# The last expert's down product in output halves, with its scatter and the last norm's first statistics between them

## What is computed

```python
def clamped_swiglu(a, u):
    a = jnp.minimum(a, SWIGLU_LIMIT)
    u = jnp.clip(u, -SWIGLU_LIMIT, SWIGLU_LIMIT)
    return a * jax.nn.sigmoid(SWIGLU_ALPHA * a) * (u + 1.0)
...
        hid = clamped_swiglu(xb @ w_gate[e] + b_gate[e], xb @ w_up[e] + b_up[e])
        yb = hid @ w_down[e] + b_down[e]
        return (yb * gt[:, None].astype(yb.dtype)).astype(t.dtype)
...
    # then, on alpha * h + moe(h), over the last axis of 1024:
    return ((tf - mu) * lax.rsqrt(var + LN_EPS) * g + b).astype(t.dtype)
```

## Time and profile before

| | us |
|---|---|
| median of 3 runs | 1060.38 (1060.24 to 1061.34) |
| span of the profiled execution | 1058.6 |
| TensorE busy | 1023.2 (97%) |
| VectorE, ScalarE, GpSimd busy | 229.8, 146.2, 28.0 |
| mean rate of all transfers | 403 GB/s |

### The profile page before, as it was taken

One profiled execution on the slowest core, in us unless ns is written; L12 is line 12 of the kernel. 1 busy time (PEld: TensorE's weight loads), 2 busy tenths in 40 slices (PEclk: granted clock), 3 DMA queues, 4 the chain that ended last, 5 costly groups with the idle time before them and its releaser, 6 DMA issues.

```text
span 1058.6 us, 12174 instructions
## 1 busy us (share of the span) xinstructions
PE 1023.2 (97%) x5124; PEld 450.5 (43%) x5124; DVE 229.8 (22%) x502; ACT 146.2 (14%) x358; POOL 28.0 (3%) x52
## 2 busy tenths in 40 slices
PE   9999999999999999999999999999999999999997
PEld 8888764333333333333333333333333333233332
DVE  5453572111111111111111112211111111111113
ACT  4311331111111111001110111111111111011102
POOL 1230100000000000000000000000000000000000
PEclk9999999999999999999999999999999999999999
DMA  9894689999999999999999999999999999999995
GB/s 315 272 414 178 210 320 407 429 427 433 431 433 430 430 428 435 433 431 432 428 435 433 428 428 432 434 430 427 431 434 431 430 431 431 436 426 425 427 418 219
DMA packets 40011, 426.21 MB, mean 403 GB/s; under 512 B 6922, under 2 KB 19347, under 8 KB 23204
## 3 DMA queue, kind: packets, MB, share of 16 engines
q1 hardware_dynamic: 37796, 423.85, 95.3%
q10 hardware_dynamic: 2176, 1.80, 0.7%
HBM read 424.59 MB, written 1.05 MB: 402 GB/s over the span
## 4 chain that ended last, share of the span: by engine, by line
PE 68%; DMA 29%; ACT 1%; DVE 1%; issue 0%; SPq 0%; POOL 0%; DVEq 0%; ACTq 0%
PE bank L1209 29%; DMA ring<-in_moe_w_up 18%; PE bank L1260 15%; DMA ring<-in_moe_w_gate 11%; PE bank L1181 4%; PE bank L1189 4%; PE bank L865 3%; PE bank L880 2%; PE bank L1055 2%; PE bank L1043 1%; PE bank L997 1%; PE bank L1251 1%; PE bank L1129 1%; PE bank L958 1%; PE bank L1063 1%; PE bank L1229 1%
## 5 line engine op out<-in xcount | busy, mean ns | idle before, releaser
L1209 PE MATMUL bank<-ring,arena 128*64 128x512 f32 x1988 | 447.9, 603 | 23.5 <-DMA ring<-in_moe_w_up 20.0
L1209 PEld LDWEIGHTS bank<-ring,arena 128*64 128x64 f32 x1988 | 142.4, 139 | 298.6 <-issue 256.8
L1260 PE MATMUL bank<-ring,arena 128*64 128x512 f32 x1024 | 226.8, 595 | 1.5 <-issue 1.5
L1260 PEld LDWEIGHTS bank<-ring,arena 128*64 128x64 f32 x1024 | 71.5, 137 | 151.7 <-issue 150.2
L1654 DVE COPY arena<-bank 128x512 f32<-128x512 f32 x32 | 22.1, 692 | 326.1 <-PE bank L1260 326.1
L746 ACT ACTIVATE arena<-arena 128x512 f32<-128x512 f32 x32 | 20.1, 629 | 450.9 <-DVE arena L1641 450.9
L1189 PE MATMUL bank<-arena 64*128 64x512 f32 x256 | 72.0, 640 | 0.9 <-DVE arena L1654 0.9
L1181 PEld LDWEIGHTS bank<-arena 128*128 128x128 f32 x480 | 58.8, 196 | 22.8 <-issue 22.8
L1648 DVE TENSOR_SCALAR arena<-bank 128x512 f32<-128x512 f32 x32 | 22.1, 691 | 210.2 <-PE bank L1209 210.2
L757 ACT ACTIVATE arena<-bank 128x512 f32<-128x512 f32 x32 | 19.1, 598 | 337.3 <-PE bank L1251 337.3
L1181 PE MATMUL bank<-arena 128*128 128x128 f32 x480 | 64.5, 288 | 0.0
(11 more groups left out here) (293 smaller groups left out, 518.5 us busy)
## 6 DMA issues: line engine op xcount, KB each, us to landing
ring<-in_moe_w_down SPq DMA_DIRECT2D x25, 4096.0 KB, 28.8
ring<-in_moe_w_gate SPq DMA_DIRECT2D x24, 4096.0 KB, 25.0
ring<-in_moe_w_up SPq DMA_DIRECT2D x24, 4096.0 KB, 27.8
ring<-in_moe_w_gate SPq DMA_DIRECT2D x10, 2048.0 KB, 22.8
ring<-in_moe_w_up SPq DMA_DIRECT2D x10, 2048.0 KB, 15.1
ring<-in_moe_w_down SPq DMA_DIRECT2D x10, 2048.0 KB, 17.3
ring<-in_w_in SPq DMA_DIRECT2D x12, 1024.0 KB, 11.8
ring<-in_moe_w_gate SPq DMA_DIRECT2D x8, 1024.0 KB, 18.2
```

The source lines that it names most:

```text
L1209: ins = mm(b[h * SL:(h + 1) * SL, :], (xA[pp], xB)[q][:, k, par * SL:(par + 1) * SL], columns(unit_at(m, kt), h), start=False, stop=kt == ...
L1260: ins = mm(bank[6][h * SL:(h + 1) * SL, :], hidT[:, kt % 4, (kt // 4) * SL:(kt // 4 + 1) * SL], unit_at(2, kt)[:, h * 512:(h + 1) * 512], ...
```

## The change

The diff, cut to what acts:

```diff
-LAST_PIECES = ((0, 2, 4, 6, 8), (0, 2, 4, 6, 7, 8), (0, 2, 4, 6, 7, 8))
+LAST_PIECES = ((0, 2, 4, 6, 8), (0, 2, 4, 6, 7, 8))
+LAST_DOWN = ((0, 3, 0, D), (3, 6, 0, 512), (6, 8, 0, 512), (3, 5, 512, D), (5, 7, 512, D), (7, 8, 512, D))
...
+                        for c, (k0, k1, c0, c1) in enumerate(LAST_DOWN):
+                            sp.dma_start(slot(s)[:, k0:k1, c0:c1], piece_src(e, m, slice(k0, k1), slice(c0, c1))).then_inc(
+                                w_landed[LAST_DOWN_AT + c] if c else landed[s], 16)
...
-            pool.wait_ge(rstd2, 1)
-            y, v, w = rstd[:, 0:1], vtmp[:, 0:1], vnew[:, 0:1]
-            link(nc.gpsimd.tensor_tensor(w, y, y, ALU.mult))
-            link(nc.gpsimd.tensor_tensor(w, w, v, ALU.mult))
-            link(nc.gpsimd.tensor_scalar(w, w, -0.5, 1.5, ALU.mult, ALU.add))
-            link(nc.gpsimd.tensor_tensor(y, y, w, ALU.mult))
-            nc.gpsimd.tensor_scalar(diag[:, :], ident[:, :], y, None, ALU.mult).then_inc(diag_ok, 1)
+            def root(y, v, n):
+                return nc.gpsimd.tensor_tensor(y, v, mhalf[0:n, :], ALU.pow)
+
+            pool.wait_ge(var2, 1)
+            link(root(rstd[:, 0:1], vtmp[:, 0:1], P))
+            nc.gpsimd.tensor_scalar(diag[:, :], ident[:, :], rstd[:, 0:1], None, ALU.mult).then_inc(diag_ok, 1)
+            pool.wait_ge(var2, 2)
+            root(rstd[:, 1:2], vtmp[:, 1:2], P).then_inc(rstd2, 1)
...
+                if last:
+                    act.wait_ge(d_ps, n)
+                    for q in range(2):
+                        act.wait_ge(hidT_ps, n + q + 1)
+                        nc.scalar.activation(hidT[:, 2 * q:2 * q + 2, :].rearrange("p c n -> p (c n)"), bank[4 + q][:, 0:2 * P],
+                                             ACT.Copy).then_inc(hidT_ok, 1)
+                    act.wait_ge(d_ps, n + 2)
+                    nc.scalar.activation(y_s[:, 256:512], bank[7][:, 0:256], ACT.Copy).then_inc(yd_ok, 1)
+                    return
...
-            nc.scalar.preload_act_table_set("natural_log_exp_and_others")
-            act.wait_ge(scat[1], nx + NE)
-            def mean_part(h):
...
+            def last_scatter(n, hh, par):
+                pe.wait_ge(yd_ok, n + 1 + hh)
+                for turn in range(2):
+                    for t in range(NT):
+                        p = t ^ turn
+                        ins = mm(bank[2 * t + hh][:, p * 256:(p + 1) * 256], selGT[par][p * SL:(p + 1) * SL, t * P:(t + 1) * P],
+                                 y_s[p * SL:(p + 1) * SL, hh * 256:(hh + 1) * 256], start=False, stop=False, skip_group_check=True)
+                        ins.then_inc(scat[t] if turn else pe_step, 1)
+                    if turn == 0:
+                        pe.wait_ge(pe_step, NT * (hh + 1))
+
+            def last_down(n, par, unit_at, arrived):
+                def part(kt, hh):
+                    arrived(2, kt, hh)
+                    for p in range(2):
+                        ins = mm(bank[6 + hh][p * SL:(p + 1) * SL, 0:256], hidT[:, kt % 4, (kt // 4) * SL:(kt // 4 + 1) * SL],
+                                 unit_at(2, kt)[:, hh * 512 + p * 256:hh * 512 + (p + 1) * 256], start=kt == 0, stop=kt == KT - 1)
+                    if kt == KT - 1:
+                        ins.then_inc(d_ps, 1)
+                pe.wait_ge(selGT_ok, n + 1)
+                pe.wait_ge(hidT_ok, n + 1)
+                for kt in range(3):
+                    if kt == 2:
+                        pe.wait_ge(hidT_ok, n + 2)
+                    for hh in range(2):
+                        part(kt, hh)
+                for kt in range(3, KT):
+                    part(kt, 0)
+                for kt in (3, 4):
+                    part(kt, 1)
+                last_scatter(n, 0, par)
+                for kt in (5, 6, 7):
+                    part(kt, 1)
+                last_scatter(n, 1, par)
...
+                    for q in range(2):
+                        pe.wait_ge(hid_ok, n + q + 1)
+                        for c in (2 * q, 2 * q + 1):
+                            ins = tr(bank[4 + q][:, (c % 2) * P:(c % 2 + 1) * P], row_group(u_c, c, 2), ident[:, :])
+                        ins.then_inc(hidT_ps, 1)
+                    last_down(n, par, unit_at, arrived)
+                    return
...
-            for t in range(NT):
-                scatter(NE - 1, t, 1)
...
+                if last:
+                    for q in range(2):
+                        at = slice(256 * q, 256 * q + 256)
+                        ins = ts(shuffled(u_c, 2)[:, q, :, :], natural(bank[5][:, :], 2)[:, q, :, :], LIMIT, -LIMIT, ALU.min, ALU.max)
+                        if q:
+                            ins.then_inc(u_ok, 1)
+                            dve.wait_ge(u_ok, n + 1)
+                        else:
+                            link(ins)
+                        stt(u_c[:, at], u_c[:, at], 1.0, a_c[:, at], ALU.add, ALU.mult).then_inc(hid_ok, 1)
+                    dve.wait_ge(d_ps, n + 1)
+                    dve.wait_ge(scat[1], n)
+                    copy(y_s[:, 0:256], bank[6][:, 0:256]).then_inc(yd_ok, 1)
+                    return
...
+            for t in range(NT):
+                dve.wait_ge(scat[t], nx + NE)
+                moments2(t, 0)
+            for t in range(NT):
+                dve.wait_ge(scat[t], nx + (NE + 1))
+                link(moments2(t, 1))
+                link(nc.vector.bn_aggr(mv[:, t, :], stats[:, 2 * t:2 * t + 2, :]))
+                ts(vtmp[:, t:t + 1], mv[:, t, 1:2], LN_EPS, None, ALU.add).then_inc(var2, 1)
```

More of the change, by code:

```diff
@@ L220, in build @@
         gsum = sm(NT)
[L221 removed]
+        eps, mhalf = sm(1), sm(1)
         gq = sm(2, 4)
@@ L744, in tile @@
             def tile(n, par, first, second, ahead, tail):
+                more, last = 1 if tail else 0, isinstance(n, int) and n == NE - 1
                 act.wait_ge(a_ok, n + 1)
@@ L1182, in gather, with scatter @@
                 ins.then_inc(gath_ps, 1)
-            def scatter(n, t, par):
+            def scatter(n, t, par, more=0):
                 pe.wait_ge(selGT_ok, n + 1)
-                pe.wait_ge(yd_ok, n + 1)
+                pe.wait_ge(yd_ok, n + 1 + more)
                 for h in range(2):
@@ L1191, in scatter, with tile @@
                 ins.then_inc(scat[t], 1)
-            def tile(n, par, first, unit_at, arrived, pp, gathers, scatters, late=None):
+            def last_scatter(n, hh, par):
[31 more added lines that the diff above has]
+                last_scatter(n, 1, par)
+            def tile(n, par, first, unit_at, arrived, pp, gathers, scatters, late=None, more=0):
                 def hidden(m, b, free, done):
                     if not first:
-                        pe.wait_ge(free, n)
+                        pe.wait_ge(free, n + (more if m == 0 else 0))
                     if not (first and m == 0):
@@ L1280, in arrived @@
                         at = ring_at(stage, UPE * k + m)
-                        if kt == 0 or (kt == 7 and is_spare(m, 0)):
+                        if isinstance(n, int) and n == NE - 1 and m == 2:
+                            for c, (k0, k1, c0, c1) in enumerate(LAST_DOWN):
+                                if kt == k0 and hh * 512 == c0:
+                                    u = LAST_DOWN_AT + c
+                                    if c:
+                                        pe.wait_ge(w_landed[u], 48 if u == 11 else 32)
+                                    else:
+                                        pe.wait_ge(landed[at % RING], it * (UPE * UNROLL // RING * 16) + (1 + at // RING) * 16)
+                        elif kt == 0 or (kt == 7 and is_spare(m, 0)):
                             pe.wait_ge(landed[at % RING], it * (UPE * UNROLL // RING * 16) + (1 + at // RING) * 16)
@@ L1633, in _, with tile @@
             copy(xcount, rank[:, 3 * NE - 1:3 * NE]).then_inc(list_ok, 1)
-            def tile(n, par, first, after, pair):
+            def tile(n, par, first, after, pair, more=0):
+                last = isinstance(n, int) and n == NE - 1
                 if pair is not None:
```

78 lines of the change are left out of this document (31 added, 47 removed).

## The result

The changed kernel takes 1065.92 us (median of 4 runs, 1065.49 to 1066.21), the kernel before 1060.52 us beside it (4 runs, 1060.24 to 1061.34). The ratio is 1.0048, with a 95% interval of 1.0036 to 1.006: slower by 5.4 us. The forecast was 1060.6 us with a range to 1061.8, and 0.06 for slower. The forecast was wrong in size: +0.2 us against a measured +5.4, and above the 1062.5 from which the prediction called it slower. That both have the same sign says little at 0.2 us. The profiled execution of the changed kernel has a span of 1064.5 us, against 1058.6.

The account below looks back on a forecast made before the run. Weight loading bounds the expert stream, so only the end moves: tile 0's last store at 1056.05, 0.5 us behind the old last store's 1055.5, landing with less company, makes +0.2 us, so 1060.6 us; range 1059.1 to 1061.8.

Parts of the forecast that it names:

- Start of down, 1038.0: After the last clamp: inner values and the 1.5 MB first weight piece let the down product start 0.5 us earlier.
- A pair in 0.22 us, 2 KB rows cost 0.05: Down product: 0.22 us per pair of 256-column matmuls; weights in 2 KB rows delay it by only 0.05 us.
- Rival (b): Down weights and scatters: 2 KB rows move at 350 GB/s and hops take 0.3 us, giving 1061.3 us; chance 0.13.
- The scatter in the middle, 1.55 us: First output half's scatter inside the down product: matmuls, shape changes, tail and hop add 1.55 us to TensorE's path.
- Second copy 1046.8, VectorE's second-half statistics 1048.9, VectorE's end 1055.3: After the product: ScalarE copies the second half, both tiles' sums follow scatter, and VectorE ends only 0.2 us earlier.
- rival (c): Last norm: GpSimd's power decides from 2.65 us on; at 5 us it gives 1063.0 us, slower; chance 0.04.
- (d): Sequencer's load hidden and both scatters cost only their matmuls: 1059.2 us, or 1058.8 with a faster-landing store; chance 0.05.
- (e): Last norm: the first half's early statistics wait and save nothing, VectorE +1.3 us, total 1061.6 us; chance 0.06.
- (a): VectorE decides the end, SP's stores last, as load is hidden or turns cheap: 1060.2 to 1059.8, down to 1059.4; chance 0.25.
- The load starts at 1048.3: gain row at 1050.1: Behind the last scatter: TensorE's count load, then 1.8 us later the matmuls putting the norm's shift row into banks.
- Diagonal matmuls at 1053.2 ... second store at 1056.05: Tile 0's end: diagonal products 3.1 us after the gain row, then ScalarE's second store, 1054.78 before.
- wrong if the gain row came before 1049: Sign against the forecast: the shift row's matmuls, expected at 1050.1, starting before 1049 would show it wrong.

Follow-up runs that it names:

- the shifted kernel: The changed kernel with 132 long-met waits added in the source in TensorE's program ahead of experts 28 to 30, shifting its last branch: 1062.17 us, ratio 1.001.
- the fastest one: The changed kernel with the added waits, the count read before the last four experts, and both last scatters behind the whole down product: 1059.59 us, ratio 0.9989.

## Why the prediction was wrong, by its own steps

*Start of down, 1038.0:* 1038.11. Right.

*A pair in 0.22 us, 2 KB rows cost 0.05:* 52 records, 13 parts, take 5.83 us; less the last one's tail of 0.16 that is 0.218 a pair. Right. No wait for a piece shows in it. The 7 us from 1036 moved 390 GB/s, between the 349 and the 419 of the earlier trace rows. Rival (b) is out.

*The scatter in the middle, 1.55 us:* 1.43 from its first matmul to the product's next (1043.87 to 1045.30). Right, 0.1 too dear (its six terms add up to 1.57, not 1.55).

*Second copy 1046.8, VectorE's second-half statistics 1048.9, VectorE's end 1055.3:* 1046.86, 1048.83, 1055.09. Right. The power on GpSimd, which had no row, takes 0.56 us: inside the bounds 0.19 and 0.60, so rival (c) is out. Rivals (d) and (e) fell with the same rows, and (a) with the last store, which is ScalarE's.

*"The load starts at 1048.3: gain row at 1050.1".* This is the step that failed. The load did start at 1048.1. The 1.8 us from it to the gain row were taken from the kernel before as a constant, and 0.35 us of them were the branch. That term was 3.35 us: 3.0 more. The gain row was only 2.3 late, because the rest was too dear: in the kernel before the branch was over at 1047.86 (1047.51 + 0.35) and the gain row stood behind the scatter's matmuls until 1048.41, and with a fast branch in the shifted kernel load to gain row took 1.4 us (1048.5 to 1049.89); the load also came 0.2 early. The prediction had asked when TensorE's sequencer gets to the load and the branch, but not where in the program the branch and its target stand. The runs show both directions: 3.35 us falls to 0.45 when code is added ahead of it, 0.35 rises to 3.8 when dead code is added behind it. Nothing in the diff's meaning tells this; it hangs on where the instructions come to stand.

*"Diagonal matmuls at 1053.2 ... second store at 1056.05".* The second failure follows from the first. All durations from the gain row on were taken from rows at clock 1.00, and the prediction never read the clock of the closing stretch as something that could change. The idle TensorE lost it, and the chain took 9.63 us instead of 5.95; with the idle time filled it took 5.87. Even without the stall it falls: in the shifted kernel, with its gaps around the last scatter, gain row to last store took 7.52 us, 1.65 more than at full clock. With two fillers ahead of the last scatter and one ahead of the gain row the same kernel kept its clock. So gaps there cost more than the time for which TensorE stands. What the wait between a scatter's two turns adds to the fall isn't shown.

*What was right of the conclusion:* with both removed the change is the same as before within 0.1% (ratio 1.0003, 0.9994 to 1.0012), by the balance that the prediction drew: VectorE's end moves from 1055.5 to 1055.09 only, and tile 0's path takes over.

*The rivals.* The slower one was put on an operation without a row, the power. The operation that did it, the branch, had a row in the kernel before (L1321, 350 ns), which stands in no term of the sum. The sign "wrong if the gain row came before 1049" looked to one side only; it came at 1052.37.

*A term inside the 3.1 us from gain row to products:* the ten `keep_clock` records (L810) between them, which the prediction carried over without pricing them. In the kernel before they ran while GpSimd wrote the diagonal until 1051.66, and cost nothing. In the changed kernel the diagonal was ready at 1051.31, before the gain row had even started, and the records stood on tile 0's path for 2.3 us at half clock (1056.07 to 1058.37); at full clock it is 1.2 (1052.44 to 1053.66 with the stall and the clock's fall removed). No run leaves them out, so what the clock would do without them isn't shown.

What stays open: which gaps of TensorE lower the clock and which do not. In the shifted kernel it fell near 1052 with TensorE's records nearly gapless since 1049.9, in the fastest one near 1051.4, gapless since 1048.1, while the kernel with the norm alone kept 1.00. And the fetched block is shown by position and by the rows of the instruction queue, not by a record that names the target's block.

## What to carry to other kernels

A branch on a register is priced by where its target lies: read the sequencer's rows of every branch on the path before and after an edit, and if one goes from tenths of a microsecond to over three, shift it by a few dozen instructions before blaming the edit. Code that never runs counts too, when it stands between a branch and its target. When an edit leaves TensorE idle near the end, price everything behind the gap at half clock as one case, and price the matmuls that would hold the clock as work on the path. Before work is put into the middle of a product, look for a gap behind the product that it could fill: here the same scatter, moved there, filled a wait of 0.48 us and made the path 0.53 us shorter.

## What the runs showed of the hardware

- A taken compare-and-branch of TensorE took 0.35 to 0.78 us (0.35 before, 0.45 shifted, 0.78 in the fastest version) in the kernels with a fast one, and 3.35 to 3.83 us in the five with a slow one; not taken, 0.08. In the slow ones a 16 KB block moved between the branch's start and its end. The Trainium skill's section named above has the mechanism, a fetch for a target outside the window, and the trace agrees with it as far as it shows blocks.
- The granted clock went to 0.50 and stayed there for some 10 us in the changed kernel (about 1050.1 to 1060.3), through 8 us of nearly unbroken matmuls. In the shifted kernel it was 0.50 from 1052 to 1055 only. Four records of 512 columns from one row took 3.77 us at 0.50 and 1.98 at 1.00.
- GpSimd's power on 128x1 takes 0.56 us, against 0.19 for its multiply.
- ScalarE's two last stores landed in 2.1 us in the changed kernel, when nothing else moved, against 2.3 for its stores and 2.7 for SP's in the earlier trace rows, and 3.5 in the kernel with the matmuls written twice.
